# A two-layer streaming trunk on one core: weight chunks loaded in pairs

## The reference, cut to what matters

```python
def peer(y, w_q, sub_keys, u, v):
    q = (yt @ w_q).reshape(T, PEER_HEADS, 2, PEER_HALF)
    s = jnp.einsum('thpc,pnc->thpn', q, sub_keys).astype(jnp.float32)
    val, idx = lax.top_k(s, PEER_TOPK)
    ...
    def block(args):
        xb, eb, gb = args
        ub = jnp.take(u, eb, axis=0)
        act = gb * jax.nn.gelu(jnp.einsum('thkd,td->thk', ub, xb), approximate=False)
        vb = jnp.take(v, eb, axis=0)
        return jnp.einsum('thk,thkd->td', act, vb)
```

## Time and profile before

| | |
|---|---|
| median of three runs | 1607.42 us (1606.4 to 1611.76) |
| the profiled execution | 1606.77 us, of which the span of instructions is 1605.0 us |
| TensorE matmul, VectorE, ScalarE, GpSimd busy | 65%, 69%, 29%, 31% of the span |
| read from HBM | 644.33 MB, 402 GB/s over the span |

### The profile page before, as it was taken

How to read it: one execution, slowest core, us unless ns; L and a number is a source line. 1 busy time by engine, 2 the same in 40 slices (tenths; PEclk the granted TensorE clock), 3 DMA queues, 4 the chain that set the end, 5 groups by cost and what they waited for, 6 DMA issues and landing times.

```text
span 1605.0 us, 19986 instructions
## 1 busy us (share of the span) xinstructions
PE 1046.8 (65%) x6936; PEld 711.0 (44%) x6936; DVE 1111.9 (69%) x3119; ACT 461.3 (29%) x953; POOL 500.8 (31%) x541
## 2 busy tenths in 40 slices
PE   8997876757734577778574477877576444544454
PEld 8995642525511266656362155665263111211111
DVE  3436878676457776997756777987765777777764
ACT  4111553111111345742111335743222111111110
POOL 0003333333223333332322323332332333333330
PEclk9998877867955699888796589877788555555666
DMA  9979999999999999999999999999999999999994
GB/s 369 408 259 402 374 420 421 417 421 420 416 420 420 421 378 415 420 415 394 422 416 420 421 411 403 417 405 374 420 418 419 421 422 421 421 421 423 420 420 190
DMA packets 105300, 646.70 MB, mean 403 GB/s; under 512 B 11632, under 2 KB 15728, under 8 KB 37616
## 3 DMA queue, kind: packets, MB, share of 16 engines
q0 software_dynamic: 76032, 553.68, 83.5%
q1 hardware_dynamic: 25536, 89.66, 14.2%
q10 hardware_dynamic: 3632, 2.08, 0.4%
HBM read 644.33 MB, written 1.05 MB: 402 GB/s over the span
## 4 chain that ended last, share of the span: by engine, by line
DMA 40%; PE 28%; DVE 15%; POOL 5%; issue 5%; ACT 4%; DVEq 2%; POOLq 0%; ACTq 0%
DMA ring<-in_uv_dram,expert 36%; PE ps L691 14%; DVE ring L1221 7%; PE ps L868 7%; POOL ring L406 5%; DMA wring<-in_wall_dram 5%; PE ps L881 2%; DVE side L1276 2%; PE ps L698 1%; PE ps L909 1%; ACT side L590 1%; PE ps L856 1%; ACT yg L471 1%; ACT osb L651 1%; ACT L475 0%
## 5 line engine op out<-in xcount | busy, mean ns | idle before, releaser
L1221 DVE CUSTOM_DVE_ANT_0 ring<-ring,ps 128x1024 f32<-128x1024 f32 x528 | 634.8, 1217 | 314.9 <-DMA ring<-in_uv_dram,expert 261.2
L406 POOL DMA_INDIRECT ring<-in_uv_dram,expert x528 | 498.7, 945 | 1068.8 <-PE ps L868 808.2
L868 PE MATMUL ps<-ring,mix 128*32 128x512 f32 x2112 | 369.3, 834 | 327.3 <-DVE mix L1237 327.3
L868 PEld LDWEIGHTS ps<-ring,mix 128*32 128x32 f32 x2112 | 67.8, 135 | 531.7 <-DVE mix L1237 391.0
L665 ACT ACTIVATE gel<-dots 128x4 f32<-128x4 f32 x132 | 27.1, 205 | 761.7 <-DVE dots L1221 761.4
L691 PE MATMUL ps<-yT,wring 128*128 128x128 f32 (+1 forms) x1184 | 159.6, 294 | 48.2 <-DMA wring<-in_wall_dram 27.6
L691 PEld LDWEIGHTS ps<-yT,wring 128*128 128x128 f32 x1184 | 150.7, 202 | 63.6 <-DMA wring<-in_wall_dram 34.2
L881 PE MATMUL ps<-sel,osb 128*128 128x16 f32 x528 | 84.1, 304 | 70.6 <-ACT osb L651 70.6
L881 PEld LDWEIGHTS ps<-sel,osb 128*128 128x128 f32 x528 | 80.7, 241 | 108.9 <-ACT osb L651 108.9
L590 ACT ACTIVATE side<-ident,params 128x128 f32<-128x128 f32 x310 | 96.3, 389 | 15.6 <-PE ps L909 14.8
L856 PE MATMUL ps<-ident,yg 128*128 128x128 f32 x264 | 48.0, 342 | 58.0 <-DVE dots L1221 58.0
(11 more groups left out here) (211 smaller groups left out, 1135.5 us busy)
## 6 DMA issues: line engine op xcount, KB each, us to landing
wring<-in_wall_dram SPq DMA_DIRECT2D x102, 512.0 KB, 11.8
ring<-in_wall_dram SPq DMA_DIRECT2D x44, 512.0 KB, 14.5
kept<-in_wall_dram SPq DMA_DIRECT2D x24, 512.0 KB, 17.0
ring<-in_uv_dram,expert POOLq DMA_INDIRECT x528, 16.1
out_dram<-fo ACTq DMA_DIRECT2D x16, 64.0 KB, 6.7
hT<-in_xT_dram ACTq DMA_DIRECT2D x1, 576.0 KB, 15.9
hT<-in_xT_dram SPq DMA_DIRECT2D x2, 256.0 KB, 3.2
params<-in_smalls_dram ACTq DMA_DIRECT2D x1, 380.0 KB, 17.7
```

The lines of the kernel that those rows point to most:

```text
L406: pool.indirect_dma_start(out=ring[:, i % R, :], out_offset=None, in_=uv, in_offset=bass.IndirectOffsetOnAxis(ap=expert[:, n % 2, k:k + 1] ...
L868: mm = pe.matmul(po[32 * j:32 * j + 32, half, :], mix[:, k, :], ring[:, slot, D + 512 * half:D + 512 * (half + 1)], start=(q == 0), stop=( ...
L1221: nc.vector.tensor_tensor_reduce(out=row, in0=row, in1=yrep, scale=1.0, scalar=0.0, op0=ALU.mult, op1=ALU.add, accum_out=dots[:, k:k + 1]) ...
```

## The change

Two neighbouring chunks of the stream become one transfer of 1 MB, 8 KB a partition. The host lays `wall` out by pairs; the two buffers of a pair are neighbours and share one semaphore; the load waits for the job of the pair's second buffer. The order of the chunks in `IN_B` changes so that pairs are neighbours in `wall`, and the gate copies of ScalarE go by chunk number. The number of buffers stays 26, that of transfers goes from 170 to 85. ScalarE's own loads are as they were.

```diff
-    IN_B = list(range(12, 24)) + list(range(8, 12)) + IN_ORDER[:8]
+    IN_B = list(range(12, 16)) + IN_ORDER[12:20] + list(range(8, 12)) + IN_ORDER[:8]
...
+        def two_at(i):
+            b = BUFFER[i] // 2 * 2
+            if b < NB:
+                return wring[:, b:b + 2, :, :].rearrange("p b c n -> p (b c n)")
+            if b >= NB + 16:
+                return kept[:, b - NB - 16:b - NB - 14, :, :].rearrange("p b c n -> p (b c n)")
+            return flat[:, (4 + b) * D:(6 + b) * D]
...
-        s_w = [sem(f"s_w{b}") for b in range(NB + 16 + KEEP)]
+        s_w = [sem(f"s_w{b}") for b in range((NB + 16 + KEEP) // 2)]
...
-            for i, (row, job) in enumerate(STREAM):
-                if BEFORE[i]:
-                    sp.wait_ge(s_proj, STREAM[BEFORE[i][-1]][1] + 1)
-                sp.dma_start(weights_at(i).rearrange("p c n -> p (c n)"), wall[row]).then_inc(s_w[BUFFER[i]], 16)
+            for i in range(0, len(STREAM), 2):
+                if BEFORE[i + 1]:
+                    sp.wait_ge(s_proj, STREAM[BEFORE[i + 1][-1]][1] + 1)
+                sp.dma_start(two_at(i), wall[STREAM[i][0] // 2]).then_inc(s_w[BUFFER[i] // 2], 16)
...
-                    dst = gate[:, k, :]
+                    dst = gate[:, IN_B[k] - 12, :]
...
-                pe.wait_ge(s_w[BUFFER[i]], 16 * (len(BEFORE[i]) + 1))
+                pe.wait_ge(s_w[BUFFER[i] // 2], 16 * (len(BEFORE[i]) + 1))
...
+    wall = wall.reshape(-1, 2, P, D).transpose(0, 2, 1, 3).reshape(-1, P, 2 * D)
```

More of the change, by code:

```diff
@@ L132, in hybrid_trunk @@
     assert all(BUFFER[LOADED[JOB["inB", k]]] == NB + k for k in range(16 + KEEP))
+    for i in range(0, len(STREAM), 2):
+        assert BUFFER[i] % 2 == 0 and BUFFER[i + 1] == BUFFER[i] + 1 and len(BEFORE[i]) == len(BEFORE[i + 1])
+        assert STREAM[i][0] % 2 == 0 and STREAM[i + 1][0] == STREAM[i][0] + 1
     ctx = ExitStack()
@@ L249, in hybrid_trunk @@
         ct = carve(AC, TA)
-        def weights_at(i):
[L252 to L257, removed]
+        def two_at(i):
[5 more added lines that the diff above has]
+            return flat[:, (4 + b) * D:(6 + b) * D]
+        def weights_at(i):
+            h = BUFFER[i] % 2
+            return two_at(i)[:, h * D:(h + 1) * D].rearrange("p (c n) -> p c n", n=P)
         ps = ctx.enter_context(nc.psum_tensor("ps", [P, 8, 512], f32))
```

## The result

| | before | after |
|---|---|---|
| median | 1608.3 us (1605.77 to 1611.92, 16 runs) | 1614.49 us (1610.95 to 1619.27, 16 runs) |
| the profiled execution | 1606.77 us, span 1605.0 | 1619.27 us, span 1617.5 |

The ratio is 1.0037, 95% interval 1.0027 to 1.0046: the change makes the kernel slower by 6.0 us (4.3 to 7.5). The forecast was +1.8 us, and the measured median lies 1.0 us above the range. The profiled execution is the slowest of the 16, so its span overstates the loss; I use it for the first phase and for rates, and the runs for the time.

The account below looks back on a forecast made before the run. The prediction took full DMA engines (bytes over rate) as the bound from about 200 us on, and TensorE in the first 113 us. Its terms, -3.4 + 1.0 + 4.2 = +1.8 us, gave 1609.2 us, range 1603.5 to 1613.5.

Parts of the forecast that it names:

- Item 4: First phase: ScalarE's load of the other tokens lands 8.6 us later beside larger weight rows, delaying all later work: +4.2 us.
- item 3: Start: the first 1 MB of weights lands some 0.3 us later for TensorE, bounds 0 and 1.2, covered by Item 4.
- Price of a packet: After 200 us: 8 KB weight rows cost the DMA engines less than two of 4 KB: -3.4 us.
- weight loads after 200 us: Where gathers have run dry, the first chunk of a burst lands later as part of a pair: +1.0 us.
- the fourth rival: Weight loads: each 8 KB row still travels as two of 4 KB, pairs land later: +2, 1609.4 us; chance 0.10.
- The tokens are held up longer: First phase: the tokens' first row also waits behind longer weight rows, +6.8 to +8.2 instead of +4.2; chance 0.20.
- Weight waits set the pace: Mixed stretches: pairs arrive faster, so 9.7 of TensorE's 29.2 us of weight waits could go: 1598.5 us; chance 0.10.
- The load isn't held up: First phase: the tokens' load doesn't share row by row, so its +4.2 us falls away: 1605.0 us; chance 0.12.
- the change does not do what it says: Same as the fourth rival: 8 KB weight rows still travel as two of 4 KB: 1609.4 us; chance 0.10.

Follow-up runs that it names:

- e6: The changed kernel with pairs of 8 KB rows only for the first 74 chunks, single chunks of 4 KB rows after; ratio to the kernel before 1.0054.
- e7: The changed kernel with the first 74 chunks single as before and pairs of 8 KB rows only from chunk 74 on; ratio to the kernel before 0.9987.
- e15: The kernel of e7 run again (first 74 chunks single, pairs from chunk 74 on); ratio to the kernel before 0.9988.
- e3: The changed kernel with the same 1 MB pairs, but each partition's 8 KB sent as two rows of 4 KB; ratio to the kernel before 1.0084.
- e1: The changed kernel with ScalarE's wait for the other tokens and their squares moved behind both halves of the scores; ratio to the kernel before 1.0016.
- e5: The changed kernel run again as it is, beside other experiments on one chip; ratio to the kernel before 1.0049.
- e8: The changed kernel with 16 idle matmuls (3.6 us) ahead of TensorE's wait for ScalarE before the second scores; ratio to the kernel before 1.0051.
- e11: The kernel of e1 run again (the change with ScalarE's token wait and squares moved later); ratio to the kernel before 1.0002.
- e16: The kernel of e12 run again (the change, first two chunks single, squares late); ratio to the kernel before 0.9980, -3.2 us.
- e12: The changed kernel with the first two chunks single and ScalarE's token wait and squares moved behind the scores; ratio to the kernel before 1.0001.
- e13: The kernel before with the other tokens loaded as 288 B rows instead of 576 B and ScalarE's parameter load issued later; ratio to before 1.0053, +8.5 us.
- e14: The kernel before with 24 idle matmuls (5.4 us) on TensorE before the second scores, DMA untouched; ratio to before 1.0041, +6.6 us.
- e4: The kernel before with one extra load of the same token bytes, into a place nobody reads, ahead of the real one; ratio to before 1.0013.
- e2: The kernel before with ScalarE's wait for the other tokens and their squares moved behind the scores; ratio to before 1.0012.

## Why the prediction was wrong

The mechanism was the right one: the tokens' late landing costs more than the larger rows save. Its price was too small. Item 4 was put at +4.2 us, with item 3 covered by it; the early half alone measured +8.7 (e6). By its own items:

1. *Price of a packet*, and 2. *weight loads after 200 us*: −3.4 and +1.0, together −2.4. Measured together, e7 −2.1 and e15 −1.9 us: right. The rates came out as worked out (420 and 421 GB/s). But as single terms they are not shown, and e3 says that they don't stand alone: pairs at a third share cost some 12 us beyond its late first gather, for which the fourth rival had +2. That the half share pays for the coarser waits would fit this; it is not shown.

3. *Start*: mis-sized. The first pair lands 8.1 us after its issue and TensorE starts at 10.10; in the six traces with an early pair of 8 KB rows and ScalarE's wait in either place (the change, e1, e5, e6, e8, e11) it starts 1.6 to 2.2 us after the 8.22, where I had 0.3 and a bound of 1.2. That it is covered by item 4 was right; where item 4 is taken away it shows, 116.95 in e1 against 115.63 in e16 at the first gather, and 116.72 in e11 against 114.99 in e12.

4. *ScalarE's load of the other tokens*: the step that failed, by size. The formula from the landing on held: L436 at 30.72 in e5 and chunk 15 by 13.1 us after that is 43.8, 5.4 us late; measured at the first gather 5.7. But the landing was taken as 29.2 and was 31.25 and 30.72: 26.5 and 26.0 us after issue instead of 24.5. The packets say why. From the first token row's start to the last one's end it took 21.2 us, where the working had 17.7 + 1.4 = 19.1: each engine moved 61 weight rows meanwhile, not 57 (19.0 us at 0.311), and its 64 token rows took 0.030 us each, 1.9 us in all. And one thing was missing altogether, TensorE's clock: after 4.00 us idle the rows show it at its lower level from 32 to 38 us, and the matmuls took 2.6 us more in the first profile and in e13. There the loss arises at the second scores, and not before chunk 15, where the formula had it; chunks 14 to 16 ran without a stop.

 So the term is 5.5 to 8.2 us at the first gather and not 4.2. In time the early half measured +8.7 us (6.6 to 10.8) in e6, 3.2 more than at its first gather. The change without idle time measured +8.2 in e8, 2.7 more, and that holds the late pairs' −2 as well. A pure delay (e14) grows less, +6.6 for 5.9. What makes up the rest is open. The traces say only where it arises: compared gather by gather with the kernel before, e6 is 5.5 us late at its first gather, 6.3 at the 289th and 9.4 at the 401st (929 and 1255 us in the kernel before), e8 5.5, 5.9 and 10.2, e14 5.9, 6.7 and 8.5. So it arises in the mixed stretches before 1255 us and not in the first phase. These are single executions, and e5, with 5.7, 4.7 and 6.7, shows little of it.

The rivals. *The tokens are held up longer*, chance 0.20 and +4.4 to +5.8 with the landing at 32 us, is nearest to what happened: 30.7 to 31.3, +6.0. Its reason, that the first row waits behind longer weight rows, is at most a small part: by the packets the first token row starts 4.0 us after the issue before, and 4.5 with the change. *Weight waits set the pace* was wrong as a gain: TensorE's waits for `wring` fell from 29.2 to 14.5 us in the changed kernel, and to 15.2 in e7, yet the late half brought 2 us, not 10. *The load isn't held up* and *the change does not do what it says* are refuted by 26.5 us and 13,296 packets. The range failed by 1.0 us at its top, because the upper bound of item 4 was given to a rival and only half taken in. Two slips of the working change nothing: the 12,768 packets are half of all, though SyncE's 1,056 were not to be halved, and the range's lower end by its own terms would be 1607.4 − 4.3 = 1603.1.

## What to carry to other kernels

When transfers share DMA engines, count rows and not bytes: making one stream's rows longer takes engine time from every stream whose rows are short, and the one to look for is the small strided load that an in-order engine waits for early in the kernel. Merging transfers can cost more than it saves (e3: +13.6 us with rows left as they were), and the two halves of a change can differ in sign (here: early +8.7, late −2.1), which only a run of each half shows. Where the work is merged, keep the phase that lives by latency as it was: that turned a loss of 0.4% into a gain of 0.1 to 0.2% in e7, e15 and e16. And look at the packet counts of an experiment's own loads: an extra load into a contiguous place (e4) has other rows than the one it is to stand for.

## What the hardware showed that was not expected

- The same 1 MB pair costs 9 to 11 us in the whole kernel if its partition row is sent as two of 4 KB (e3 against e1), though the rates of e3 and of the change differ by only 1%: 417 and 421 GB/s in 420 to 460 us. By the rates that is 3.5 us over the 96 chunks after 200 us (item 1 of the prediction); what the rest is, share between queues or place in HBM, no run separates.
- Two queues share a DMA engine row by row: 1,038 packets of the one and 1,036 of the other in the same 11 us, of 4 KB and of 576 B.
- TensorE's matmuls ran at half speed after 1.88 us idle (e5, the first of the six chunks from 10.38) and after 4.00 us (the change), yet after 1.82 us at the same place in another execution they ran at full speed (10.96 us for the same six). Idle time alone doesn't decide it at the start: the six took 12.86 us in e6 after 1.18 us idle, and without any idle time just before them 10.95 (e12) to 11.88 us (e2). The granted clock reads 0.50 behind the 4.00 us; in e5 it reads 1.00 from 8 to 16 us while only 29 matmuls ended there against 56.

The two stretches, the change first, then e5 (busy us and count of each engine, clock, DMA share, GB/s):

```profile
8.00:16.00 8.00, 6.17 (x56) 6.01 (x55) 1.80 (x4) 1.65 (x2) 0.00 (x0) 1.00 1.01 416
```

```profile
8.00:16.00 8.00, 6.12 (x29) 5.85 (x28) 1.24 (x2) 1.65 (x2) 0.00 (x0) 1.00 1.02 418
```
